# Encoder layer with a bidirectional S5 scan: scan parameters in the memory stage, tiles asked for by their reader, the scan's states in pairs of slots, y split and last activation moved

## What is computed

```python
def hybrid_mixer(xn, ...):
    proj = xn @ w_in
    u_s5, x_c, gate_b, gate_c, g = split(proj)
    gates = sigmoid(g + b_gate)
    u = u_s5.reshape(bsz, L, 32, 16)                  # 32 groups of 16 channels, 64 complex states each
    y = s5_direction(u, ..., reverse=False) + s5_direction(u, ..., reverse=True)
    y = gelu(y.reshape(bsz, L, 512) + s5_d * u_s5)
    s5_out = (y @ w_glu_a) * sigmoid(y @ w_glu_b)
    z = gate_c * x_c
    conv_out = (gate_b * conv3(z)) @ w_conv_out
    return (gates[..., :1024] * s5_out + gates[..., 1024:] * conv_out) @ w_o

def s5_direction(u, a_re, a_im, log_dt, b, c, reverse):
    A_bar = exp(A * exp(log_dt)); B_bar = ((A_bar - 1) / A) * B
    h[t] = A_bar * h[t-1] + B_bar @ u[t]              # associative scan over the rows
    return real(C @ h)

h = x + mixer(rmsnorm(x)); h = h + cross_attention(rmsnorm(h), rmsnorm(mem)); h = h + swiglu(rmsnorm(h))
```

## Time and profile before

| | us |
|---|---|
| median of three runs | 2540.95 (2539.57 to 2541.70) |
| the profiled execution | 2542.96 |
| its span in the trace | 2541.3 |
| PE busy | 2451.0 (96%) |
| DVE busy | 1641.1 (65%) |
| ACT busy | 765.8 (30%) |
| POOL busy | 275.4 (11%) |
| mean granted clock of PE | 0.988 |

### The profile page before, as it was taken

The page is one execution under the profiler, slowest core; times in us unless marked ns, Lnnn a source line. Parts: engine busy times, 40 slices in busy tenths (PEclk is TensorE's granted clock), DMA queues, the critical chain, the costliest instruction groups (busy, mean ns, idle before and its releaser), DMA issues.

```text
span 2541.3 us, 34409 instructions
## 1 busy us (share of the span) xinstructions
PE 2451.0 (96%) x12542; PEld 2201.0 (87%) x12542; DVE 1641.1 (65%) x2978; ACT 765.8 (30%) x1226; POOL 275.4 (11%) x283
## 2 busy tenths in 40 slices
PE   8999988799999999999999999999999999999997
PEld 6788866678888788888868999999999999999996
DVE  6735542358874397253264588888878687777777
ACT  5301110232222332130143244343343343332333
POOL 0078781000000021000000000010100000000000
PEclk9999998999999999999999999999999999999999
DMA  7332227542223743213231212132332621222212
GB/s 240 120 116 82 84 71 140 147 142 73 73 82 125 206 182 124 83 58 133 81 107 49 87 50 76 59 113 85 110 104 94 250 68 58 88 82 79 77 69 73
DMA packets 103801, 262.99 MB, mean 103 GB/s; under 512 B 15104, under 2 KB 46336, under 8 KB 103680
## 3 DMA queue, kind: packets, MB, share of 16 engines
q1 hardware_dynamic: 96736, 238.82, 29.1%
q0 software_dynamic: 6944, 22.55, 2.6%
HBM read 198.45 MB, written 64.98 MB: 104 GB/s over the span
## 4 chain that ended last, share of the span: by engine, by line
PE 88%; DVE 3%; DMA 2%; issue 1%; ACT 1%; SPq 0%; DVEq 0%; ACTq 0%
PE bank L735 27%; PE bank L737 27%; PE bank L736 27%; PE bank L1013 2%; PE bank L959 2%; PE bank L990 1%; DMA BBL<-scratch_BB 1%; PE bank L956 1%; PE bank L1002 0%; DVE EL L2133 0%; ACT EH L1176 0%; DVE HR L2446 0%; PE bank L901 0%; DMA ML<-scratch_M 0%; SPq L413 0%
## 5 line engine op out<-in xcount | busy, mean ns | idle before, releaser
L735 PE MATMUL bank<-XN,WLO 128*128 128x512 f32 x1152 | 449.3, 390 | 3.7 <-DVE WLO L1639 1.7
L737 PE MATMUL bank<-XN,WHI 128*128 128x512 f32 x1152 | 448.2, 389 | 0.0
L736 PE MATMUL bank<-XN,WHI 128*128 128x512 f32 x1152 | 448.2, 389 | 0.0
L735 PE MATMUL bank<-XH,EL 128*128 128x384 f32 x1232 | 412.4, 335 | 1.6 <-DVE U2T L2159 0.9
L737 PE MATMUL bank<-XH,EH 128*128 128x384 f32 x1232 | 411.5, 334 | 0.0
L736 PE MATMUL bank<-XL,EH 128*128 128x384 f32 x1232 | 411.5, 334 | 0.0
L735 PEld LDWEIGHTS bank<-XN,WLO 128*128 128x128 f32 x1152 | 216.2, 188 | 50.2 <-issue 3.1
L736 PEld LDWEIGHTS bank<-XN,WHI 128*128 128x128 f32 x1152 | 216.2, 188 | 45.1 <-issue 0.5
L737 PEld LDWEIGHTS bank<-XN,WHI 128*128 128x128 f32 x1152 | 216.2, 188 | 45.0
L735 PE MATMUL bank<-AF,EL 128*128 128x384 f32 x704 | 238.3, 338 | 9.7 <-DVE AF L1644 6.4
L736 PE MATMUL bank<-AF,EH 128*128 128x384 f32 x704 | 236.5, 336 | 0.0
(11 more groups left out here) (267 smaller groups left out, 3888.4 us busy)
## 6 DMA issues: line engine op xcount, KB each, us to landing
RAW<-W_all SPq DMA_DIRECT2D x132, 512.0 KB, 3.5
WR<-W_all SPq DMA_DIRECT2D x92, 512.0 KB, 4.5
scratch_G<-GS SPq DMA_DIRECT2D x16, 768.0 KB, 3.7
XS<-xT SPq DMA_DIRECT2D x8, 768.0 KB, 6.0
scratch_CO<-COS SPq DMA_DIRECT2D x8, 768.0 KB, 4.3
COL<-scratch_CO SPq DMA_DIRECT2D x8, 768.0 KB, 4.3
G2L<-scratch_G SPq DMA_DIRECT2D x8, 768.0 KB, 5.8
G1L<-scratch_G SPq DMA_DIRECT2D x8, 768.0 KB, 7.2
```

Of the source, the lines that this page charges most:

```text
L735: pe_mm(out, w[1], x[0], start=first, stop=False, skip_group_check=onto)
L736: pe_mm(out, w[0], x[1], start=False, stop=False, skip_group_check=onto)
L737: return pe_mm(out, w[0], x[0], start=False, stop=last, skip_group_check=onto)
```

## The change

- `parameters` 0 and 1 stand in the memory stage behind slot 6's work, 2 behind slot 11's, 3 and 4 behind slot 13's and 5 and 6 behind slot 15's, ahead of values_out(1). The sines stand on ACT between slots 12 and 13.
- POOL asks for BX to CY of the first direction before its first instruction, for BX and BY of the second behind B_bar's store, and for CX and CY at the second's start.
- SP asks for VN(it+2) when VN(it) has been transposed, and for WK and BBL(it+2) when the lags of `it` are out. The first two pairs are asked for in co's third slot.
- H is [98 pairs, 64, 2]: slots 2k and 2k+1 of one group are neighbours (4 bytes apart), pairs are 512 bytes apart. Every reader and writer of H follows; copies of states go in four pieces (even and odd slots) instead of two. SBUF tiles behind H move by half a KB.
- s5b: one ML matmul of all 192 columns per group, then WO·H as before; its banks are 4 to 7, and PE waits for the gelu of four pairs of groups back.
- y: SP loads y by half tiles, quad by quad. k = 0 is split during s5b, behind the ninth gelu, into XN's last tile; glu's last merged_hi waits until all readers of it are through. YL lies at 0.
- FFN: in the last step of each group `gated`, `act_hi` and `gated_lo` of the first half of columns stand one or two products earlier (`close`).

The core of the diff:

```diff
@@ SBUF
-    H = at("H", 0, [SLOTS, GD])
+    H = at("H", 0, [PAIRS, GD, 2])
+    YL = low("YL", 0, [HT, C, NC])
@@ SP
+            if j == 2:
+                for par in range(2):
+                    sp.wait_ge(S(f"tables_stored{par}"), 2 * 4 * 32)
+                sp.wait_ge(S("bb_stored"), 32)
+                for par in range(2):
+                    load_v(par, par)
+                    load_w(par, par)
...
-                if not (last and par):
-                    sp.wait_ge(S("states_bwd"), it)
-                    s5a_loads(it + 1, 1 - par)
+                if not last:
+                    sp.wait_ge(S("v_turned"), it + 1)
+                    load_v(it + 2, par)
+                    sp.wait_ge(S("lags"), it + 1)
+                    load_w(it + 2, par)
...
         for q in range(quads):
+            if q:
+                load_y(q - 1)
             sp.wait_ge(S("y_made"), 2 * (q + 1))
             sp.dma_start(Y_d[:, g, :], U[:, g, :]).then_inc(S(f"y_stored{q // 2}"), 16)
             if q + 2 < quads:
                 s5b_loads(q + 2)
-            if q % 2 == 0 and q:
-                load_y(q // 2 - 1)
-        sp.wait_ge(S("y_lo"), HT)
@@ POOL
+        for dst, src in ((BX, "BX"), (BY, "BY"), (CX, "CX"), (CY, "CY")):
+            pool.dma_start(dst[:], io[src][0]).then_inc(S("bc_in"), 16)
...
+            if d == 0:
+                for dst, src in ((BX, "BX"), (BY, "BY")):
+                    pool.dma_start(dst[:], io[src][1]).then_inc(S("bc_in"), 16)
@@ PE, s5b
-                        pe.wait_ge(S("y_made"), 2 * (q - 1) + n + 1)
-                    out = PS[2 * par + n][:, g % 2 * NC:(g % 2 + 1) * NC]
-                    for c0, n, slot in ((0, NCP, 0), (NCP, NCS, SLOT_S)):
-                        o = out[:, c0:c0 + n]
-                        nc.tensor.matmul(o, ML[par][:, g, :], u[:, c0:c0 + n], start=True, stop=False)
-                        for d in (1, 0):
-                            h = H[:, slot:slot + n, bass.ds(d * GROUPS + QUAD * q + g, 1)].rearrange("p s o -> p (s o)")
+                        pe.wait_ge(S("y_made"), 2 * q + n - 3)
+                    out = PS[4 + 2 * par + n][:, g % 2 * NC:(g % 2 + 1) * NC]
+                    nc.tensor.matmul(out, ML[par][:, g, :], one(U, QUAD * q + g), start=True, stop=False)
+                    for d in (1, 0):
+                        for c0, n, slot in ((0, NCP, 0), (NCP, NCS, SLOT_S)):
+                            h = H[:, slot // 2:(slot + n) // 2, bass.ds(d * GROUPS + QUAD * q + g, 1), :]
@@ ACT, s5a (DVE's copies likewise) and y
-        for lo, n, c in ((1, NCP, 0), (SLOT_S + 1, NCS, NCP)):
-            copy(dst[:, :, lo:lo + n], src[:, :, c:c + n]).then_inc(signal, 1)
+        for slot, n, c in ((0, NCP, 0), (SLOT_S, NCS, NCP)):
+            for odd in range(2):
+                dst = states_of(d * GROUPS + 2 * it, slot, n, odd)
+                copy(dst, src[:, :, c + odd:c + n:2]).then_inc(signal, 1)
...
+            if it == GROUPS // 4:
+                y_split(0)
...
+                if isinstance(i, int) and par:
+                    act.wait_ge(res, RES0["glu"] + 6 * KT)
@@ DVE
+            if n == 6:
+                parameters(0)
+                parameters(1)
+            if n == KT + 3:
+                parameters(2)
             if n == KT + 4:
                 values_out(0)
+            if n == KT + 5:
+                parameters(3)
+                parameters(4)
+            if n == 2 * KT - 1:
+                parameters(5)
+                parameters(6)
...
-            def seqs(a, s, p0=0, p1=P):
-                a = a[p0:p1, bass.ds(s, SLOT_S + 1 if both else 1), :]
-                return a[:, ::SLOT_S, :] if both else a
+            def seqs(s, p0=0, p1=P):
+                a = H[p0:p1, bass.ds(pair + s // 2, SLOT_S // 2 + 1 if both else 1), :, s % 2]
+                return a[:, ::SLOT_S // 2, :] if both else a
...
                 if j == 5:
                     with_first(UP1, 3, U3T, (S("summed"), 5 * s + 2), j, s)
+                    if close:
+                        gated(s, 0)
                 if j == 6:
+                    if close:
+                        gated_lo(s, odd, 0)
                     with_first(G2T, 2, U2T, (S("summed"), 5 * s + 1), j, s)
```

More of the change, by code:

```diff
@@ L285, in key_bank, with states_of, y_part @@
         return PS[n % 4]
+    def states_of(g, slot, n, odd):
+        pairs = slice((slot + 1 + odd) // 2, (slot + 1 + odd) // 2 + n // 2)
+        return H[:, pairs, bass.ds(g, 2), 1 - odd].rearrange("p s g -> p g s")
+    def y_part(low, k):
+        return YHL[:, low, k] if k else XN[:, low, KT - 1]
     def xo_bank(j, b):
@@ L458, in _, with load_y @@
         y_rows = Y_d.rearrange("(t p) g c -> g p t c", p=GP)
-        def load_y(k):
-            sp.wait_ge(S(f"y_stored{k}"), 32)
-            for g in range(P // GP):
+        def load_y(q):
+            k, half = q // 2, q % 2
+            sp.wait_ge(S(f"y_stored{k}"), 16 * (half + 1))
+            for g in range(4 * half, 4 * half + 4):
                 sp.dma_start(YL[GP * g:GP * (g + 1), k], y_rows[8 * k + g]).then_inc(S(f"y_in{k}"), 16)
@@ L1318, in _, with y_split, glu @@
             gate(i)
+        def y_split(k):
+            act.wait_ge(S(f"y_in{k}"), 128)
+            copy(y_part(0, k).rearrange("p (c t) -> p c t", t=C), YL[:, k].rearrange("p t c -> p c t")
+                 ).then_inc(S("y_hi"), 1)
         for it in range(GROUPS // 2):
             act.wait_ge(S("s5_out"), it + 1)
-            nc.scalar.activation(U[:, 2 * it:2 * it + 2, :], PS[it % 4][:, 0:2 * NC].rearrange(
+            nc.scalar.activation(U[:, 2 * it:2 * it + 2, :], PS[4 + it % 4][:, 0:2 * NC].rearrange(
                 "p (g c) -> p g c", g=2), ACT.Gelu_apprx_tanh).then_inc(S("y_made"), 1)
-        for k in range(HT):
-            act.wait_ge(S(f"y_in{k}"), 128)
-            copy(YHL[:, 0, k].rearrange("p (c t) -> p c t", t=C), YL[:, k].rearrange("p t c -> p c t")
-                 ).then_inc(S("y_hi"), 1)
-        with loop(nc.scalar, 4) as i:
+            if it == GROUPS // 4:
+                y_split(0)
+        for k in range(1, HT):
+            y_split(k)
+        def glu(i):
             for par in range(2):
@@ L1340, in _ @@
                     copy(one(XN[:, 0], j)[:, blk(b)], SB[:, blk(b)]).then_inc(S("merged_hi"), 1)
+        with loop(nc.scalar, 3) as i:
+            glu(i)
+        glu(3)
         def residual(name, norm):
@@ L1809, in _ @@
             dve.wait_ge(S(f"kv_stored{par}"), 128)
-        for part in range(5):
-            parameters(part)
         for j in range(4):
@@ L1901, in _ @@
         for slot in (0, SLOT_S):
-            then(V.memset(H[:, slot, :], 0.0))
+            then(V.memset(H[:, slot // 2, :, 0], 0.0))
         def s5a(i):
@@ L1951, in advance, with gates @@
             dve.wait_ge(scan.sem, scan.n)
-        def gates(i, both, slot, steps):
+        def gates(i, both, pair, steps):
             for par in range(2):
@@ L1963, in gates @@
                 for s in range(steps[par]):
-                    advance(slot + steps[0] * par + s, both is not False)
+                    advance(pair, steps[0] * par + s, both is not False)
         gates(0, "first", 0, (8, 8))
@@ L2016, in _ @@
                 merged_lo(NB - 1)
-            step.leave(4)
+        with loop(V, 3) as i:
+            step.enter(i, 2 * NB)
+            glu(i)
+            step.leave(3)
+        glu(3)
         def add_squares(norm, k, sq):
```

142 lines of the change are left out of this document (70 added, 72 removed).

## The result

The changed kernel takes 2496.48 us (median of 4 runs, 2494.89 to 2500.30), the kernel before 2541.32 beside it: a ratio of 0.9826, 95% interval 0.9809 to 0.9843. It is 45 us faster; 64 were forecast. The profiled execution took 2497.11, its span is 2494.4. The direction was right, and the time lies 1.5 above the upper end of the range (2495).

What follows compares the result with a forecast made beforehand. TensorE was taken as the bound (PE busy 96% of the span). Terms summing to −63.9 us took the profiled 2542.96 to 2479.1, or 2477 on the median of 2540.95; range of 8 in 10: 2464 to 2495.

Steps and rivals of the forecast that it cites:

- Conv: Conv: earlier scan parameters and loads let POOL end at 366.6, removing PE's 22.23 us wait and slow clock; −23.5 us.
- s5a: First pass of the scan part: tiles requested earlier remove PE's waits on BBL, stage 53.8 us; −16.5 us taken.
- s5b: Paired slots and one ML matmul of 192 make a group 0.98 instead of 1.76, then loads bind; −10 us.
- Rival B: s5b and s5a: PE waits before almost each quad, the clock stays near 0.51, s5b gains nothing; 2489 us, chance 0.18.
- The scan: Gate stage: DVE's five operations per step on every second fp32 cost no more; 0 us.
- rival E: Gate stage: the stride slows DVE's scan operations by over 0.13 us each and eats all gains; 2552 us, chance 0.02.
- y: y stage: k=0 split during s5b lets PE start at once, with 2.2 us idle before k=1; −5.7 us.
- Last activation, first group: End of the first FFN group: making the first half earlier cuts PE's 4.51 us wait for AF and slow clock; −6.1 us.
- Second group: End of the second FFN group: the same earlier first half removes PE's 1.9 us wait; −1.9 us.
- Rival A: s5b: pairs read no faster than single slots, so it keeps −2 of its −10; 2485 us, chance 0.12.
- C: s5a: the load queue binds, landings of over 4 us use up the 0.8 us of cover; 2483 us, chance 0.08.
- D: Conv: POOL still late, starting at 125 instead of 117.8, and the slow clock stays; 2484 us, chance 0.10.

Runs made afterwards that it cites:

- e1: The changed kernel with the seven scan parameters and two sines back in their old place, POOL's early loads kept: 2510.11 us, ratio 0.9874.
- e8: The changed kernel with y's k=0 split behind the last gelu, like k=1 to 3: 2504.53 us, ratio 0.9854.
- e6: The changed kernel with all YL loads behind the last quad, and so y's k=0 split behind the last gelu: 2503.32 us, ratio 0.9851.
- e3: The changed kernel with H laid out by single slots again, all else unchanged: 2499.97 us, ratio 0.9835.
- e15: The changed kernel with each group's ML as two matmuls of 128 and 64 columns again, pairs of slots kept: 2496.78 us, ratio 0.9819.
- e7: The changed kernel with WO and ML of quad q+2 asked for ahead of the gelu and y's store: 2497.45 us, ratio 0.9823.

## Why the prediction was wrong, step by step

- **Conv** (−23.5, measured −22.3 with a new wait of 1.0 in co): right in mechanism, place and numbers; e1 shows it. Of its two parts POOL's start came 1.3 later than forecast and its chain 0.5 shorter.
- **u** (−0.2, measured −0.6): right.
- **s5a** (−16.5, measured −18.0): right; the 53.8 of the working was nearer than the rounded-down value taken.
- **s5b** (−10, measured −1.6): the loads bind, as forecast, and pairs read at twice the speed; the step that failed is the walk through the quads, in three terms. "ML lands 3.9 to 5.5 (median 4.8) after" is a median over loads with and without YL loads behind them. The same change puts YL loads beside nearly each ML, and it lands after 5.7 to 6.2, so the way from a quad's end to the quad after next takes 7.6 to 8.0 and not 6.4, 4.0 over three rounds (1.4 and 4.8 add to 6.2; no row is named for the rest of the 6.4). The group (0.98, measured 1.22) is another 3.0 in quads 3, 5 and 7. The slow clock "behind the other waits" (2.4) measured 6.4 in the same three quads. Against that quad 1 was 1.2 cheaper than forecast, and the 1.3 given back for y_split(0) wasn't needed (e8). Without the YL loads 7.6 of the 8.4 come back (e6), a part of the slow clock with them.
- **Rival B** named the clock: every second quad ran slow, and s5b gained next to nothing, as it said. It was wrong on the extent: quads 2, 4 and 6, ahead of which PE doesn't wait, run at 1.00, and so does the y stage's start.
- **The scan** (0): right. The first of its operations takes 292 and 224 ns, 290 and 224 before, in the lines of DVE over the gate stage below; the rise that rival E needs (over 0.13 us) isn't there.

```profile
L1989 DVE TENSOR_TENSOR S<-H,LR 128x128 f32<-128x128 f32 x64 | 18.7, 292 | 1.9
...
L1989 DVE TENSOR_TENSOR S<-H,LR 128x64 f32<-128x64 f32 x64 | 14.4, 224 | 2.0
```

- **y** (−5.7, measured −6.8): right.
- **Last activation, first group** (−6.1, measured +1.3): the 5.6 came, and the step that failed is that the gain was carried to the end with nothing behind it. The earlier PE meets the next weights, which land when they did: 4.2 of wait at U2T and 2.5 of slow clock. The transfers behind it were already full, and PE's old wait was their slack.
- **Second group** (−1.9, measured −2.2): right.
- **Attention** (0, measured +3.5): taken at nothing because the change doesn't touch it; the fetch of PE's code was foreseen by no case, and no row shown of before points to it.

s5b, the first FFN group and attention together fell 8.4 + 7.4 + 3.5 = 19.3 short; the other terms gave 2.1 more than forecast, so that the traces have 46.8 of the 63.9. Rival A (2485) would have missed as well: pairs do read twice as fast. C and D did not occur.

## What to carry to other kernels

When a change moves several things, read each landing time with the change's own new transfers in the queue: here the YL loads of one good edit took 7.6 us from another, each costed alone, and giving each quad its own tiles and each transfer its turn brought them back. A median over loads with and without such company is the price of neither. Where a wait of the bounding engine goes, look further on (here 20 us) for the transfer that was on time only because of it; a queue at full rate gives nothing back, but its order can be changed. A stage whose tiles are fewer than its latency needs doesn't get faster by faster matmuls.

## What was not expected of the hardware

- fp32 columns that PE reads in pairs of 4-byte neighbours, the pairs 512 bytes apart, go at the contiguous rate: 0.23 for 128 columns against 0.43 for single ones 256 bytes apart (changed kernel and e3). What the Trainium skill ("SBUF — State Buffer", Specifications (TRN2)) says of two hits on a line is borne out by this; DVE's operations on every second fp32 cost no more than contiguous ones (292 against 290 ns).
- One packet of instructions (0.02 MB) stands among the 144 of a store in each kernel in which that store lands after 5.1 to 5.7 and not 3.3, and one matmul more or less per group of s5b in PE's code, 400 us earlier, decides whether it is there (e15).
- The length of a wait alone doesn't tell what the clock does behind it. Behind waits of 2.5 to 3.5 us in the changed kernel, and of 1.5 in the kernel before, the granted clock was 0.50 to 0.70 for 3 us and more. But in e7 PE ran a quad at 1.00 behind a wait of 2.6, and in e6 two behind waits of 1.4 and 1.1.
